# Weighted sum of gathered expert rows: four 64x64 TensorE products per slot in place of two 128x128, halves put back by ScalarE

## The reference

```python
def blk(xb):                                   # a block of 128 tokens
    q = (xb @ w_q).reshape(PEER_BLOCK, PEER_HEADS, 2, PEER_DK // 2)
    s1 = jnp.einsum('thd,hnd->thn', q[:, :, 0], keys[0]).astype(jnp.float32)
    s2 = jnp.einsum('thd,hnd->thn', q[:, :, 1], keys[1]).astype(jnp.float32)
    v1, i1 = lax.top_k(s1, PEER_TOPK)
    v2, i2 = lax.top_k(s2, PEER_TOPK)
    ...                                        # the 16 best of 16 x 16 sums, and their experts
    g = jax.nn.softmax(sc, axis=-1)
    act = jax.nn.gelu(jnp.einsum('thkd,td->thk', u[eidx], xb).astype(jnp.float32))
    return jnp.einsum('thk,thkd->td', (g * act).astype(v.dtype), v[eidx])
```

## Time and profile before

| what | us |
|---|---|
| median of 3 runs | 4593.08 (4584.23, 4593.08, 4607.25) |
| the profiled execution, its span | 4588.8 |
| both PEER stages together, from their first gather | 781.7 to 2500.0 and 2844.45 to 4588.8 |
| PE busy, DVE busy, ACT busy, POOL busy | 3744.7, 3181.0, 967.0, 1511.0 |

### The profile page before, as it was taken

One profiled execution on the slowest core, in us unless ns is written; L12 is line 12 of the kernel. 1 busy time (PEld: TensorE's weight loads), 2 busy tenths in 40 slices (PEclk: granted clock), 3 DMA queues, 4 the chain that ended last, 5 costly groups with the idle time before them and its releaser, 6 DMA issues. The chain is left out here.

```text
span 4588.8 us, 42624 instructions
## 1 busy us (share of the span) xinstructions
PE 3744.7 (82%) x10383; PEld 1787.6 (39%) x10383; DVE 3181.0 (69%) x7667; ACT 967.0 (21%) x2243; POOL 1511.0 (33%) x1316
## 2 busy tenths in 40 slices
PE   7688888878787878788877988878787878787877
PEld 2266565333333333333333544333333333333332
DVE  6533343778777777777887353778778778787787
ACT  5432141111111111111122341111111111111112
POOL 0000000344444444444443000344444444444443
PEclk9899869989899999899998999989898989898999
DMA  8410004999999999999997104899999999999998
GB/s 330 177 48 28 34 0 171 360 412 384 408 399 396 401 396 398 397 397 399 406 414 315 59 27 166 348 411 377 402 393 391 404 390 404 388 407 384 401 420 351
DMA packets 206990, 1467.85 MB, mean 320 GB/s; under 512 B 24280, under 2 KB 29160, under 8 KB 35688
## 3 DMA queue, kind: packets, MB, share of 16 engines
q0 software_dynamic: 184320, 1342.26, 72.3%
q1 hardware_dynamic: 21684, 121.29, 7.0%
q10 hardware_dynamic: 828, 2.76, 0.2%
HBM read 1462.84 MB, written 3.38 MB: 320 GB/s over the span
## 5 line engine op out<-in xcount | busy, mean ns | idle before, releaser
L785 PE MATMUL peer_acc<-peer_ring,peer_diag 128*128 128x512 f32 x5120 | 2505.4, 638 | 634.6 <-DVE peer_diag L651 634.3
L438 POOL DMA_INDIRECT peer_ring<-in_uv,peer_index x1280 | 1498.7, 1171 | 2515.2 <-PE peer_acc L785 1738.2
L785 PEld LDWEIGHTS peer_acc<-peer_ring,peer_diag 128*128 128x128 f32 x5120 | 988.5, 202 | 1923.4 <-issue 1000.8
L643 DVE CUSTOM_DVE_ANT_0 peer_ring<-peer_ring,HY 128x1024 f32<-128x1024 f32 x1280 | 1557.9, 1218 | 139.1 <-issue 62.5
L509 ACT ACTIVATE peer_acts<-peer_dots 128x1 f32<-128x1 f32 x1280 | 258.6, 203 | 2793.2 <-DVE peer_dots L643 2792.6
L651 DVE TENSOR_SCALAR peer_diag<-ident,peer_acts,peer_gate 128x128 f32<-128x128 f32 x1280 | 438.0, 342 | 61.9 <-PE peer_acc L785 42.2
L738 PE MATMUL peer_qp<-HT,peer_wq 128*128 128x512 f32 (+1 forms) x896 | 294.9, 453 | 0.0
L738 PEld LDWEIGHTS peer_qp<-HT,peer_wq 128*128 128x128 f32 x896 | 182.4, 204 | 241.3 <-issue 241.3
L564 DVE MAX8 peer_best<-peer_sc 128x8 f32<-128x128 f32 x160 | 40.3, 289 | 331.9 <-PE peer_sc L753 331.4
L657 DVE TENSOR_TENSOR peer_tmp<-peer_acc,peer_G 128x1024 f32<-128x1024 f32 x80 | 98.0, 1224 | 91.2 <-PE peer_acc L785 84.8
L702 PE MATMUL peer_acc<-peer_ring,HY 128*128 128x512 f32 x320 | 142.6, 607 | 15.7 <-DMA peer_ring<-in_w_out 15.7
(11 more groups left out here) (280 smaller groups left out, 2958.9 us busy)
## 6 DMA issues: line engine op xcount, KB each, us to landing
mod_wmod<-in_w_mod SPq DMA_DIRECT2D x16, 2048.0 KB, 8.9
peer_ring<-in_uv,peer_index POOLq DMA_INDIRECT x1280
HT<-in_w_mod SPq DMA_DIRECT2D x8, 2048.0 KB, 9.2
peer_wq<-in_w_q SPq DMA_DIRECT2D x16, 1024.0 KB
peer_ring<-in_w_out SPq DMA_DIRECT2D x8, 1024.0 KB, 8.8
lru_wlru<-in_w_lru SPq DMA_DIRECT2D x4, 2048.0 KB, 7.7
hgrn_wqvg<-in_w_hgrn_qvg SPq DMA_DIRECT2D x4, 1536.0 KB, 6.5
peer_ring<-scratch_mod_rows SPq DMA_DIRECT2D x12, 512.0 KB, 14.3
```

Source lines behind the costliest of these rows:

```text
L438: pool.indirect_dma_start(ring[:, j % SLOTS, :], None, uv[:, :], bass.IndirectOffsetOnAxis(ap=index[:, j:j + 1], axis=0), element_offset=l ...
L643: dve.tensor_tensor_reduce(u, u, H[:, j // TOPK, :], 1.0, 0.0, ALU.mult, ALU.add, dots[:, j:j + 1]).then_inc(dot_done, 1)
L785: last_mm = pe.matmul(acc[b % 2][:, lo:lo + 512], diag[:, j % NDIAG, :], ring[:, j % SLOTS, D + lo:D + lo + 512], start=(e == 0), stop=(e ...
```

## The change

The v half of a slot is no longer multiplied with the whole 128x128 `diag`. It is cut into token halves `r` (partitions 0 to 63 and 64 to 127) and column halves `c` (512 each). Since `diag` is diagonal, token half r needs only the 64x64 block of `diag` with the same rows and columns. That gives four products with a contraction of 64, 64 outputs, and 512 moving columns. The product (r, c) reads partitions of half r, and is written to PSUM partitions of half c, in bank r. So `acc` holds the unit's result with token and column halves exchanged in place. ScalarE puts them back with four 64x512 copies into `tmp` (`unpack`), at s = 3 of the next unit, and for the last unit at the end of the head. `add_unit` now reads `tmp` in SBUF. TensorE waits for `unpacked` instead of `added` before it uses an accumulator again, and its two waits stand apart.

```diff
+HALF = P // 2
...
+        added, unpacked = sem(pre + "added"), sem(pre + "unpacked")
...
+                act.sem_inc(unpacked, 1)
...
+                def unpack(h, b):
+
+                    act.wait_ge(slot_free, h * PER_HEAD + ((b + 1) * TOPK + SLOTS))
+                    act.wait_ge(added, h * NB + (b + 1))
+                    for r in range(2):
+                        for c in range(2):
+                            last_copy = act.activation(tmp[r * HALF:(r + 1) * HALF, c * 512:(c + 1) * 512],
+                                                       acc[b % 2][c * HALF:(c + 1) * HALF, r * 512:(r + 1) * 512], ACT.Copy)
+                    last_copy.then_inc(unpacked, 1)
...
                         act.activation(acts[:, j:j + 1], dots[:, j:j + 1], ACT.Gelu_apprx_tanh).then_inc(act_done, 1)
+                        if s == 3 and b:
+                            unpack(h, b - 1)
...
+                    unpack(h, NB - 1)
...
                 def add_unit(h, b):
 
-                    dve.wait_ge(slot_free, h * PER_HEAD + ((b + 1) * TOPK + SLOTS))
-                    dve.tensor_tensor(tmp[:, :], acc[b % 2][:, :], G2[:, cond_of(b), :], ALU.mult).then_inc(tmp_done, 1)
+                    dve.wait_ge(unpacked, h * NB + (b + 2))
+                    dve.tensor_tensor(tmp[:, :], tmp[:, :], G2[:, cond_of(b), :], ALU.mult).then_inc(tmp_done, 1)
...
-                        pe.wait_ge(added, h * NB + (1 if b == 0 else b))
+                        wait_apart(pe, unpacked, h * NB + (1 if b == 0 else b))
                         for e in range(TOPK):
                             j = b * TOPK + e
-                            pe.wait_ge(diag_done, h * PER_HEAD + (j + 1))
-                            for lo in (0, 512):
-                                last_mm = pe.matmul(acc[b % 2][:, lo:lo + 512], diag[:, j % NDIAG, :],
-                                                    ring[:, j % SLOTS, D + lo:D + lo + 512],
-                                                    start=(e == 0), stop=(e == TOPK - 1))
+                            wait_apart(pe, diag_done, h * PER_HEAD + (j + 1))
+                            for c in range(2):
+                                for r in range(2):
+                                    rows = slice(r * HALF, (r + 1) * HALF)
+                                    last_mm = pe.matmul(acc[b % 2][c * HALF:(c + 1) * HALF, r * 512:(r + 1) * 512],
+                                                        diag[rows, j % NDIAG, rows],
+                                                        ring[rows, j % SLOTS, D + c * 512:D + (c + 1) * 512],
+                                                        start=(e == 0), stop=(e == TOPK - 1), skip_group_check=True)
                             last_mm.then_inc(slot_free, 1)
```

More of the change, by code:

```diff
@@ L370, in body @@
         dot_done, act_done, diag_done = sem(pre + "dot_done"), sem(pre + "act_done"), sem(pre + "diag_done")
-        added = sem(pre + "added")
+        added, unpacked = sem(pre + "added"), sem(pre + "unpacked")
         wq_in, keys_in = sem(pre + "wq_in"), sem(pre + "keys_in")
```

## The result

The changed kernel takes 4534.74 us (median, 4532.41 to 4538.77) where the kernel before took 4593.47 us in the same session. The ratio is 0.9867, with a 95% interval of 0.9851 to 0.9883. It is faster by 58.7 us, less than half of the 129 us forecast. The profiled execution took 4533.8 us against 4588.8, so it shows 55.0 us of the gain.

A forecast was written before the change was run, and what follows sets the result against it. VectorE and TensorE set the pace in turn, with transfers close behind. Steady transfers save 174 us, head ends give back 49, stage ends gain 4: -129 us, so 4464 us; range 4410 to 4565.

The forecast's parts named there:

- Side by side: Weighted sum on TensorE: a slot's four small products run all together, 0.85 us a slot at full clock.
- matmuls start and end strictly in program order: Rival for TensorE's weighted sum: rows keep program order across tiles, a slot stays 1.71 us, 4662 us; chance 0.07.
- Transfers become the bound: PEER stages: VectorE's head falls to 191.5 or 200 us, under the 202.8 us that transfers need at 421 GB/s.
- 415 and 206 were the signs of being right: Signs that the forecast holds: repeated heads near 206 us at about 415 GB/s.
- The clock: TensorE idles more between slots, so its granted clock falls well below 0.91, often to 0.5; sign: under 0.85.
- The second rival: Side by side, but slow clock keeps TensorE behind in the 48 slots with queries; 4515 to 4570 us, chance 0.13.
- VectorE: Within a head: score waits 24.1 to 5-12 us, `diag` wait of 2.5 gone, head's end 5.5 to 3.6, jump stays 5.8.
- 12.2 + 1.6: Head's end: VectorE stops 12.2 us after one dot and diagonal of 1.6 us.
- ScalarE: Within a head, the four copies, 2.4 us, hide under `route_b` on VectorE; uncovered, up to 2.4 us in four units.
- I take 3.5 us for each of 14 ends, 49 us: Head ends: transfer time lost because gathers start late, between 2 us and 5 us with slow clock and queries.
- 174: Both PEER stages after their first units: 78.6 and 95.4 us saved by a steady flow at 421 GB/s.
- a gain of 4: The stages' own ends: 1.9 us gained at each, 4 us in all.

The follow-up runs named there:

- e4: The changed kernel with four of the 16 query steps in each repeated head: 4522.73 us.
- e3: The changed kernel with the last unit's `add_unit` moved from the head's end to s = 7 of the next head's first unit: 4534.5 us.
- e16: The changed kernel with the head loop written out on every engine and the last unit's `add_unit` moved into the next head: 4480.04 us.
- e6: The changed kernel with the head loop written out on every engine: 4477.28 us.
- e13: The changed kernel with the head loop written out on VectorE alone, plus four reductions at each head end but the last: 4502.56 us.
- e9: The changed kernel with the head loop written out on VectorE alone: 4488.1 us.
- e15: The changed kernel with VectorE's head loop written out and half of each dot product left out: 4471.16 us.
- e17: The changed kernel with VectorE's head loop written out, plus a loop of two rounds over one tiny reduction at each head end but the last: 4492.7 us.
- e18: The changed kernel with VectorE's loop alone as head 0, three rounds of two heads, then the last head: 4515.18 us.
- e8: The changed kernel with all four 64x64 products of a slot on the same tile: 8862.57 us.
- e1: The kernel before with each 128x128 product as two of full contraction and 64 outputs, TensorE's two waits standing apart: 4644.84 us.
- e14: The changed kernel, jump kept, plus four reductions on VectorE at each head end but the last: 4535.89 us.

## Why the prediction was right in kind and wrong in size

**Side by side.** Right. Rows of the weighted sum in the changed kernel's timeline, at the end of a head and in a window inside layer 0:

```profile
3470.90 1.95 PE L802 MATMUL peer_acc<-peer_ring,peer_diag 64*64 64x512 f32 x16 [1.38 <-DVE peer_diag L666]
3472.78 0.71 PE L768 MATMUL peer_sc<-peer_keys,peer_qT 128*128 128x128 f32 x4
...
1400.33 3.52 PE L802 MATMUL peer_acc<-peer_ring,peer_diag 64*64 64x512 f32 x16 [2.72 <-DVE peer_diag L666]
```

16 rows are two slots. From 3470.90 to the scores at 3472.78, at a granted clock of 1.00, they take 0.94 us a slot, where 0.85 was forecast, and in the second case, at a granted clock of 0.54, 1.76 us a slot. All four tiles work at once. The Trainium skill's rule that matmuls start and end strictly in program order ("TensorE: Matmul & The Clock Gate", The mechanism), taken for each row, would have made a slot 1.71 us at full clock; the trace does not agree with it across tiles. Nor do starts follow the program for whole products there: in the earlier trace rows the second block's first product starts ahead of the first block's second one. So that each engine executes its instructions in written order, as the kernel's description has it, is not so for TensorE across tiles.

**Transfers become the bound.** Right in kind: VectorE waits 21.2 us of a head for gathers instead of 0.6. But the stages run at 406 to 408 GB/s and the repeated heads take some 209 us, where 415 and 206 were the signs of being right.

**The clock.** Right: 0.76 to 0.78 in the stages against 0.92 and 0.93 in the earlier trace rows. That TensorE is still fast enough there is what e4 says: with 12 of 16 queries gone only 12 us are gained. The second rival had half of the gain, some 50 us, on a TensorE that falls behind in the slots with queries, so that the time came out in its range was chance.

**VectorE.** Right where the waits within a head are concerned: the score waits became 0.9 us (5 to 12 forecast) and `diag`'s went. The head's end took 4.0 us here, but 5.2 in the mean where 3.6 was forecast, so next to nothing of the 1.9 us came. The jump took 4.5 (5.8). In all the first dot stands 14.1 us behind the last one at the 12 ends, close to the 12.2 + 1.6 of the prediction, though its own terms, 3.6, two times 1.2 and 5.8, add to 11.8 and not 12.2. First dot to GpSimd's next gather took 3482.32 to 3487.88 = 5.56 us (5.5 forecast).

```profile
3482.32 1.22 DVE L658 CUSTOM_DVE_ANT_0 peer_ring<-peer_ring,HY 128x1024 f32<-128x1024 f32 x1 [4.50 <-issue]
...
3487.88 1.56 POOL L439 DMA_INDIRECT peer_ring<-in_uv,peer_index  x1 [12.92 <-PE peer_acc L802]
```

**ScalarE.** Right within a head. In the timeline of ScalarE the copies stand in their place, and VectorE is inside `route_b` meanwhile:

```profile
3525.38 0.20 ACT L521 ACTIVATE peer_acts<-peer_dots 128x1 f32<-128x1 f32 x1 [1.20 <-DVE peer_dots L658]
3525.61 2.40 ACT L501 ACTIVATE peer_tmp<-peer_acc 64x512 f32<-64x512 f32 x4
```

**The sum: where it failed.** The mis-sized term is "I take 3.5 us for each of 14 ends, 49 us". It measured 108 us, 7.7 for each end if all of it is put on the ends, and 8.1 in the one head shown above. The saving was therefore 174 - 108 = 66 us, as the two stretches show (65.8), and not 125. The second miss is the 10.8 us outside them, where I had counted a gain of 4; 2.9 of these lie ahead of both stages. Together 59 + 15 = 74 us, which is 129 - 55.

I had derived the 3.5 us from a ring that runs dry because VectorE comes late: the first gather in time, later ones about 2 us late, 5 us with a slow clock and queries in the way. The lateness came as reckoned (14.1 us, and 5.56 to GpSimd's gather). The step that failed is the next one, from the lateness to the transfers that are lost: no row of before stood behind it, and the loss was over twice as large, in windows 2 to 32 us behind the first dot. Nor does it follow the lateness. In layer 1 of e3 VectorE is 5.4 us earlier at the first dot and 3.1 at the ninth, in e16 7 us earlier at the first than in e6, and nothing is gained. e13 leaves VectorE nearly as late as the jump did, and 32 of 47 us stay gained.

What the experiments took of the 108 us, inside the stages: 36.5 go away with VectorE's loop, of which 16.5 are what e13's delay costs. 10.4 more go when the loops of the other engines are written out too (e6), though GpSimd's and TensorE's bring nothing there alone. 12.1 are VectorE's dots, from e9 to e15. If these add, some 50 us are left that no experiment took away.

**What stays open.** Why VectorE's long loop costs 32 us more than a delay in place of its stop, 20 of them inside the stages. It isn't any jump (e17). The 0.8 us by which VectorE is less late in e13 could be part of it. The stop itself goes with a load of instructions. At a head's end of the changed kernel, with the first dot at 3693.2, the DMA queues show for 3682 to 3695:

```profile
q0 software_dynamic: 751, 5.47, 101.4%
q14 instruction: 1, 0.01, 0.2%
```

In 13 us around the same first dot in e9 and in e13 (3648 to 3661, 3658.9 to 3671.9) there is only the first of these queues. At all six such ends of layer 1 this packet, 8 KB, starts 2.1 us before the first dot, and two more follow, 2.9 and 10.4 us behind it. In layer 1 of e18 such a packet stands there only at the two ends with a long jump. That loading them takes time from the gathers would fit a cost that goes with long jumps. But a packet takes 0.33 us of one of 16 DMA engines, and the page counts only 1.02 MB in one instruction queue and 1.54 MB in the other for the changed kernel, and 0.76 and 1.54 MB for e9, too little to fill 8 us a head by volume. So this cause of the rest of the loop's price isn't shown, and what makes the 50 us isn't either.

## What to carry to other kernels

Before a change is credited with the time that a bound leaves, take the loop out once, on one engine at a time: here that was worth as much as the change itself (57 us against 59), and on one engine 47 us. Read inside the changed stages too, since 9 of these 47 us stood ahead of them. An engine's stop at a jump in the profile (4.5 us) is neither its price nor additive: work ahead of it hides in it, and what the transfers lose is another number. When you forecast "the transfers become the bound", read how they recover from each interruption in windows of 10 us, since a residual that is small at one end (7.7 us) takes 108 of the 174 us over 14 ends.

## What the hardware showed beyond that

Four 64x64 fp32 tiles with different rows and columns ran fully side by side: eight rows of 512 columns in 0.94 us at a granted clock of 1.00 and 1.76 at 0.54, against 6.9 us on one tile at 0.50 (e8). Two 128x64 ones did so too (e1).

TensorE's granted clock did not follow its busy share. On one tile it was busy 190.58 of 200 us and had 0.50, and 0.664 over the run with 96% busy; with whole products it was busy for 82% and stood at 0.92 and 0.93 in the stages. e8 paid twice, for its rows one behind another and for the clock.

A stop of 4.5 us behind a long jump on VectorE was nearly filled by 4.2 us of other work ahead of the jump (e14: 0.5 us of it were left), and a jump over one short instruction had no stop at all (e17). In layer 1 a packet of an instruction queue, 8 KB, starts 2.1 us ahead of the first dot behind each long jump.
